# Low parts of the up-projection's weights made by accumulating DMAs instead of GpSimd subtractions

## The chip, the core and the metric

The kernel runs on one core of a Trainium2 chip. Time is the device time of one execution in microseconds (us). The core's engines are TensorE (PE in the profile; its weight loads are PEld), VectorE (DVE), ScalarE (ACT), GpSimd (POOL) and SyncE (SP). They run side by side and wait for each other on semaphores. SBUF is the memory on the core, PSUM holds the results of TensorE.

## What is computed

One layer of a decoder trunk for a prompt of 512 tokens and 8 single tokens, so 520 columns of activations. The part that the change touches is the feed-forward network at its end:

```python
def conv_ffn(h, w_up, conv_w, conv_b, w_down, buf):
    z = h @ w_up                                   # (tokens, 2048) @ (2048, 2 * 5632)
    zp = jnp.concatenate([buf.astype(z.dtype), z], axis=1)
    zc = conv_b + sum(zp[:, j:j + T] * conv_w[j] for j in range(CONV_W))
    g, a = jnp.split(zc, 2, axis=-1)
    y = (jax.nn.silu(g) * a) @ w_down              # (tokens, 5632) @ (5632, 2048)
    return y, zp[:, -(CONV_W - 1):]
```

Ahead of it stand a projection of the normed input, three mixers (a gated MLP, an attention with a window, an mLSTM memory) and an output projection. All arrays are float32.

## The kernel before

**Products in two parts.** TensorE multiplies in the rounded format fp32r. To keep the precision, both sides are split: `whi` is the weight rounded, `wlo` what is left (`raw - whi`), and `h2_hi` and `h2_lo` are the same for the activations. A product is then three: hi x hi, hi x lo of the activations, and lo of the weights x hi (`tile_mm`, line 507; its matmuls have line 514).

**Units and quarters.** An up unit is 128 columns of `w_up`: 2048 x 128 weights, 1 MB. SP loads it into one of the two slots of `raw` (`load_pair`, line 2139 and `load_after`, line 2254). A unit has four quarters of 128 x 512 weights each. `whi` and `wlo` have room for four quarters, a ring: quarter k of each unit stands in place k. Quarter k takes the rows 4c + k of the 16 blocks of 128 rows (`rawq`, a strided view). For each quarter

- ScalarE waits until TensorE has read the place (`w_used`) and writes `whi` (`q_hi`, line 1034, which raises `w_hi`),
- GpSimd waits for `w_hi` and writes `wlo = raw - whi` (`up_split`, line 2107, or `split_pairs`, line 2070; both raise `w_lo`),
- TensorE waits for `w_lo` and runs 24 matmuls of 128 x 260 (`up_mm`): 3 products x 4 blocks x 2 halves of the columns.

A down unit is a block of `w_down` worked in seven pieces of 12 matmuls (`down_unit`, line 913). ScalarE (line 1360) and GpSimd (line 2115) prepare its pieces in the same ring, some of them from `sums` that VectorE makes of the raw blocks (line 1863).

**Order.** The 5632 hidden channels go in 11 groups. Group 0 has eight up units. Groups 1 to 9 are a loop, each with eight up units of its own and the four down units of the group before, in the order `SEQ`. The last group has an order of its own, `SEQ_LAST`, and its down units at the end.

```python
SEQ = ("u0", "u1", "d0", "u2", "d1", "u3", "d2", "u4", "d3", "u5", "u6", "u7")
```

Each unit of this order uses the slot of `raw` given by its place, even or odd. A unit's load is started when the low parts of the unit two places ahead of it are made, because GpSimd is the last reader of `raw`. Seven pieces do not divide by four, so behind a down unit the ring is shifted: place 0, which quarter 0 of the next up unit needs, was last used by the fifth piece, place 1 by the sixth and place 2 by the seventh.

ScalarE and VectorE also do the convolution, the gate and the splitting of the gated activations between the quarters, at places that a table in `ffn_group_act` (`due`) fixes: `start_g` (line 1338), `start_a` (line 1343), `silu`, `gated_hi`, `mixed_hi`.

## Time and profile before

| | before |
|---|---|
| median of 2 runs | 2183.91 us (2182.3 to 2185.52) |
| the profiled execution's span | 2180.7 us |
| TensorE matmuls | 2158.9 us busy, 99% |
| VectorE | 1332.5 us, 61% |
| ScalarE | 820.2 us, 38% |
| GpSimd | 1153.8 us, 53% |
| DMA | 213.66 MB, 34.5% of the 16 engines' span on the main queue |

The busy time of an engine is the time in which it runs instructions. Matmuls are pipelined and their ends are modelled, so two that follow each other overlap in the records; the distance between their starts is the better measure. A line of a group gives its count, its busy time with the mean of one in ns, and the idle time just ahead of its instructions with what ended it. The times in the timeline are from the span's start.

### The profile page before, as it was taken

To read this page: it belongs to the slowest core of one execution; us is meant where nothing else is said; L and a number is where in the kernel's file an instruction comes from. 1 tells how busy PE (TensorE), PEld (TensorE's weight loads), DVE (VectorE), ACT (ScalarE), POOL (GpSimd) and SP (SyncE) were. 2 spreads that over 40 slices of the span, in tenths; PEclk is the share of its full clock that TensorE was granted. 3 is DMA by queue.
4 is the path that set the end of the run, shared out by engine and by line. 5 is a ranking of instruction groups with operands and counts; after the bars stand their busy time and mean duration, and the time that the engine had idled before them with its cause. 6 is when DMAs were issued, how large, how long until landed. Compare 5 with 4: busy or idle time off the path is not lost.

```text
span 2180.7 us, 45547 instructions
## 1 busy us (share of the span) xinstructions
PE 2158.9 (99%) x17888; PEld 2103.8 (96%) x17888; DVE 1332.5 (61%) x1872; ACT 820.2 (38%) x1394; POOL 1153.8 (53%) x868
## 2 busy tenths in 40 slices
PE   7999999999999999999999999999999999999999
PEld 7999988988899999999999999999999999999999
DVE  6122347266643577676785767767677676867765
ACT  5223342255444333333333333333333333333331
POOL 5443333332244457566565765656667575665652
PEclk9999999999999999999999999999999999999999
DMA  7532233752232423323333333233423333333323
GB/s 221 139 91 68 76 75 81 112 158 67 64 88 67 120 78 107 101 84 105 89 96 98 96 98 96 86 96 89 117 77 103 91 96 98 96 96 91 105 81 124
DMA packets 325112, 213.66 MB, mean 98 GB/s; under 512 B 12760, under 2 KB 299473, under 8 KB 324113
## 3 DMA queue, kind: packets, MB, share of 16 engines
q1 hardware_dynamic: 322153, 211.28, 34.5%
q10 hardware_dynamic: 2880, 1.26, 0.3%
q8 instruction: 58, 0.95, 0.2%
q14 instruction: 21, 0.17, 0.0%
HBM read 201.38 MB, written 11.49 MB: 98 GB/s over the span
## 4 chain that ended last, share of the span: by engine, by line
PE 92%; issue 3%; POOL 2%; ACT 1%; DMA 1%; DVE 1%; POOLq 0%; SPq 0%; ACTq 0%; DVEq 0%
PE ps L514 57%; PE ps L913 18%; PE ps L791 8%; PE ps L893 2%; POOL wlo L2070 1%; PE ps L831 1%; PE ps L851 1%; PE ps L841 1%; DMA xtok<-in_x_prompt 0%; PE ps L632 0%; ACT act_hi L1065 0%; DMA raw<-in_w_in 0%; PE ps L478 0%; PE ps L989 0%; PE ps L642 0%
## 5 line engine op out<-in xcount | busy, mean ns | idle before, releaser
L2107 POOL TENSOR_TENSOR wlo<-raw,whi 128x512 fp32r<-128x512 f32 x336 | 467.5, 1399 | 356.9 <-ACT whi L1034 345.2
L1034 ACT ACTIVATE whi<-raw 128x512 fp32r<-128x512 f32 x552 | 340.6, 629 | 727.7 <-PE ps L514 475.5
L2070 POOL TENSOR_TENSOR wlo<-raw,whi 128x512 fp32r<-128x512 f32 x200 | 259.6, 1300 | 443.0 <-ACT whi L1034 443.0
L514 PE MATMUL ps<-h_hi,whi 128*128 128x260 f32 x2816 | 395.7, 283 | 0.0
L514 PE MATMUL ps<-h_lo,whi 128*128 128x260 f32 x2816 | 393.8, 282 | 0.0
L514 PE MATMUL ps<-h_hi,wlo 128*128 128x260 f32 x2816 | 393.2, 282 | 0.0
L514 PEld LDWEIGHTS ps<-h_hi,whi 128*128 128x128 f32 x2816 | 360.9, 188 | 0.4
L514 PEld LDWEIGHTS ps<-h_lo,whi 128*128 128x128 f32 x2816 | 360.8, 188 | 0.0
L514 PEld LDWEIGHTS ps<-h_hi,wlo 128*128 128x128 f32 x2816 | 360.6, 188 | 0.0
L2115 POOL TENSOR_TENSOR wlo<-sums,whi 128x512 fp32r<-128x512 f32 x160 | 215.1, 1344 | 159.6 <-ACT whi L1360 154.8
L1360 ACT ACTIVATE whi<-sums 128x512 fp32r<-128x512 f32 x160 | 101.2, 632 | 269.5 <-PE ps L514 256.7
L913 PE MATMUL ps<-g_hi,whi 128*128 128x260 f32 x1120 | 179.3, 282 | 1.2 <-DVE qacc L1845 1.0
L913 PE MATMUL ps<-g_lo,whi 128*128 128x260 f32 x1120 | 180.4, 283 | 0.0
L2115 POOL TENSOR_TENSOR wlo<-raw,whi 128x512 fp32r<-128x512 f32 x120 | 172.7, 1440 | 13.6 <-ACT whi L1360 8.0
L913 PE MATMUL ps<-g_hi,wlo 128*128 128x260 f32 x1120 | 179.0, 282 | 0.0
L913 PEld LDWEIGHTS ps<-g_hi,whi 128*128 128x128 f32 x1120 | 152.6, 188 | 1.6 <-ACT whi L1034 1.2
L913 PEld LDWEIGHTS ps<-g_lo,whi 128*128 128x128 f32 x1120 | 153.8, 188 | 0.0
L913 PEld LDWEIGHTS ps<-g_hi,wlo 128*128 128x128 f32 x1120 | 153.0, 188 | 0.0
L514 PE MATMUL ps<-act_hi,whi 128*128 128x260 f32 x960 | 141.4, 290 | 0.7 <-POOL wlo L2070 0.7
L1893 DVE TENSOR_TENSOR za<-ps,rs 128x520 f32<-128x520 f32 x44 | 30.8, 700 | 178.8 <-PE ps L514 178.8
L514 PE MATMUL ps<-act_lo,whi 128*128 128x260 f32 x960 | 135.5, 284 | 4.0 <-DVE act_lo L1486 2.4
L514 PEld LDWEIGHTS ps<-act_hi,whi 128*128 128x128 f32 x960 | 124.4, 189 | 10.8 <-issue 9.2
(363 smaller groups left out, 3054.9 us busy)
## 6 DMA issues: line engine op xcount, KB each, us to landing
raw<-in_w_up SPq DMA_DIRECT2D x88, 1024.0 KB, 5.8
raw<-in_w_down SPq DMA_DIRECT2D x44, 1024.0 KB, 5.0
raw<-in_w_in SPq DMA_DIRECT2D x30, 1024.0 KB, 5.6
raw<-in_w_out SPq DMA_DIRECT2D x64, 256.0 KB, 3.8
x_spill<-xT SPq DMA_DIRECT2D x1, 4160.0 KB, 16.1
xtok<-in_x_prompt SPq DMA_DIRECT2D x4, 1024.0 KB, 8.4
out_y_prompt<-ytok SPq DMA_DIRECT2D x3, 1024.0 KB
xT<-x_spill SPq DMA_DIRECT2D x1, 2860.0 KB, 9.4
```

The lines of the kernel that those rows point to most:

```text
L514: mm = nc.tensor.matmul(ps[:, bank + h, 0:NH], w[:, k, c, :], x[:, 4 * c + k, h * NH:(h + 1) * NH], start=(k == 0 and kind == 0 and c == 0 ...
L791: mm = nc.tensor.matmul(ps[:, b + h, 0:NH], w[:, k, c, :], x[:, p, 4 * half + c, h * NH:(h + 1) * NH], start=(half == 0 and kind == 0 and ...
L831: mm = nc.tensor.matmul(ps[:, 4 + r, lo:256], zT[64 * r:64 * r + 64, Z_BQ + u, i * P:(i + 1) * P], keys[:, (i - 1) * P + lo:(i + 1) * P], ...
L841: t = nc.tensor.transpose(ps[:, 6, (2 * r + kb) * P:(2 * r + kb + 1) * P], sx[:, n % 4, r, kb * P:(kb + 1) * P], ident[:])
L893: mm = nc.tensor.matmul(ps[:, b + h, 0:NH], w[:, k, c, :], x[:, h, E_SLOT[c], :], start=(kind == 0 and c == 0), stop=(kind == 2 and c == 3))
L913: mm = nc.tensor.matmul(ps[:, bank + g, 0:NH], w[:, k, 2 * i + g, :], x[:, i, BLOCKS[p], :], start=(kind == 0 and i == 0), stop=(kind == 2 ...
L1034: nc.scalar.activation(whi[:, k, :, :], rawq(k, slot), ACT.Copy)\
L1360: nc.scalar.activation(ring(whi, p % 4), down_weights(p, slot), ACT.Copy).then_inc(w_hi, 1)
L1893: tt(halves(z[:, 2:]), pair(bank), halves(rs2[:]), mult).then_inc(z_free, 1)
L2070: nc.gpsimd.tensor_tensor(wlo[:, k, :, :], rawq(k, u), whi[:, k, :, :].bitcast(F32), ALU.subtract).then_inc(w_lo, 1)
L2107: nc.gpsimd.tensor_tensor(wlo[:, k, :, :], rawq(k, u % 2), whi[:, k, :, :].bitcast(F32), ALU.subtract).then_inc(w_lo, 1)
L2115: nc.gpsimd.tensor_tensor(ring(wlo, k), down_weights(p, slot), ring(whi, k).bitcast(F32), ALU.subtract).then_inc(w_lo, 1)
```

## The change

For the up units u1 to u7 of group 0 and of the nine loop groups, the low part is made in another way. ScalarE writes the rounded quarter into `whi` and the same quarter, rounded and negated, into `wlo` (`signed_hi`). GpSimd then raises `w_lo` by a nop and issues a DMA that adds the raw quarter onto `wlo` in SBUF (`up_add`). Each of the four places has its own semaphore `low_added[k]` for the landing. TensorE waits for it ahead of the quarter, and SP waits for all four before it loads over that slot of `raw`. u0 of each group, the last group and all down units keep the subtraction on GpSimd.

The quarter of these units is now four neighbouring blocks (`raw4`, contiguous in each row of SBUF, 2 KB) instead of every fourth one; `tile_mm` takes the blocks of the activations to match (`four_by_k`). To have semaphores for it, four others are merged with those of the input's loads (`X_LOADED`); this moves no instruction.

```diff
+    low_added = [sem(f"low_added{k}") for k in range(4)]
...
+    def raw4(k, s):
+
+        return raw[:, s, 4 * k * P:4 * k * P + 4 * P].rearrange("p (c n) -> p c n", c=4)
...
-    sems = {}
+    X_LOADED = 16
+    sems = {"kc_in": x_in[0], "vc_in": x_in[1], "b_in": x_in[2], "c_in": x_in[3]}
...
-                                              x[:, 4 * c + k, h * NH:(h + 1) * NH],
+                                              x[:, 4 * k + c if four_by_k else 4 * c + k, h * NH:(h + 1) * NH],
...
-        def up_mm(q0, bank, before=None):
+        def up_mm(q0, bank, before=None, added=None):
             for k in range(4):
                 pe.wait_ge(w_lo, q0 + (k + 1))
                 if before is not None:
                     before(k)
-                tile_mm(k, bank, whi, wlo, h2_hi, h2_lo)
+                if added is not None:
+                    pe.wait_ge(low_added[k], added)
+                tile_mm(k, bank, whi, wlo, h2_hi, h2_lo, four_by_k=added is not None)
...
+        def signed_hi(q, k, slot, landed):
+
+            if k == 0:
+                act.wait_ge(raw_in[slot], landed)
+            act.wait_ge(w_used, q + 1)
+            nc.scalar.activation(whi[:, k, :, :], raw4(k, slot), ACT.Copy)
+            nc.scalar.activation(wlo[:, k, :, :], raw4(k, slot), ACT.Copy, scale=-1.0).then_inc(w_hi, 1)
...
+        def up_add(q, slot):
+
+            for k in range(4):
+                pool.wait_ge(w_hi, q + (k + 1))
+                begun(pool)
+                pool.engine_nop().then_inc(w_lo, 1)
+                nc.gpsimd.dma_start(wlo[:, k, :, :].bitcast(F32), raw4(k, slot), accum_op=ALU.add).then_inc(low_added[k], 16)
...
+        up_split(4 * U_FFN, 0)
+        for u in range(1, U_GRP):
+            up_add(4 * (U_FFN + u), u % 2)
...
-                (down_split if name[0] == "d" else up_split)(q0 + Q_AT[name], at % 2)
+                (down_split if name[0] == "d" else up_add if at else up_split)(q0 + Q_AT[name], at % 2)
...
+                if with_down and older[0] == "u" and older != "u0":
+                    begun(sp)
+                    for k in range(4):
+                        sp.wait_ge(low_added[k], low_count(grp, int(older[1])))
+                        begun(sp)
```

On ScalarE, in the loop behind the down unit d0, before (line 1360 is the last piece of d0, line 1034 the quarters of u2, line 1343 a step of the convolution):

```order
L1360 ACTIVATE whi<-raw 128x512 [waits w_used]
L1033 REGISTER_ALU [waits raw_in1]
L1034 ACTIVATE whi<-raw 128x512 [waits w_used]
L1343 ACTIVATE ca<-za,cpar 128x520 [waits f_za]
L1033 REGISTER_ALU
L1034 ACTIVATE whi<-raw 128x512 [waits w_used]
```

And of the changed kernel at the same place (lines 1395 and 1396 are the two instructions of `signed_hi`):

```order
L1373 ACTIVATE whi<-raw 128x512 [waits w_used]
L1394 REGISTER_ALU [waits raw_in1]
L1395 ACTIVATE whi<-raw 128x512 [waits w_used]
L1396 ACTIVATE wlo<-raw 128x512
L1356 ACTIVATE ca<-za,cpar 128x520 [waits f_za]
L1394 REGISTER_ALU
L1395 ACTIVATE whi<-raw 128x512 [waits w_used]
L1396 ACTIVATE wlo<-raw 128x512
```

The second instruction of each quarter stands directly behind the first and ahead of the step of the convolution.

On GpSimd, at the same place in the loop, before (line 2115 is the last piece of a down unit, line 2107 the quarters of the up unit behind it):

```order
L2114 REGISTER_ALU
L2115 TENSOR_TENSOR wlo<-raw,whi 128x512 [waits w_hi]
L2106 REGISTER_ALU
L2107 TENSOR_TENSOR wlo<-raw,whi 128x512 [waits w_hi]
L2106 REGISTER_ALU
L2107 TENSOR_TENSOR wlo<-raw,whi 128x512 [waits w_hi]
```

And now (line 2134 is the nop that raises `w_lo`, line 2135 the DMA):

```order
L2152 REGISTER_ALU
L2153 TENSOR_TENSOR wlo<-raw,whi 128x512 [waits w_hi]
L2132 REGISTER_ALU
L2134 ISA [waits w_hi]
L2135 DMA wlo<-raw 128x512
L2132 REGISTER_ALU
L2134 ISA [waits w_hi]
L2135 DMA wlo<-raw 128x512
```

A nop and a DMA stand where one subtraction stood.

On TensorE, the start of the up unit behind the down unit, before (line 913 is the last piece of the down unit, line 514 the quarters):

```order
L913 MATMUL ps<-g_hi,wlo 128x260 x3
L967 REGISTER_ALU
L877 REGISTER_ALU [waits z_free,d_ev]
L514 MATMUL ps<-h_hi,whi 128x260 [waits w_lo]
L514 MATMUL ps<-h_hi,whi 128x260 x7
L514 MATMUL ps<-h_lo,whi 128x260 x8
L514 MATMUL ps<-h_hi,wlo 128x260 x8
```

And now:

```order
L925 MATMUL ps<-g_hi,wlo 128x260 x3
L979 REGISTER_ALU
L887 REGISTER_ALU [waits z_free,d_ev]
L891 ISA [waits w_lo]
L524 MATMUL ps<-h_hi,whi 128x260 [waits low_added0]
L524 MATMUL ps<-h_hi,whi 128x260 x7
L524 MATMUL ps<-h_lo,whi 128x260 x8
L524 MATMUL ps<-h_hi,wlo 128x260 x8
```

The wait for the landing stands ahead of the first of the 24 matmuls; the eight that read `wlo` are the last.

## Rows read from the trace of the kernel before

**Rows 1.** The page's part 1: engine, busy us, share of the span, instructions

```profile
PE 2158.9 (99%) x17888; PEld 2103.8 (96%) x17888; DVE 1332.5 (61%) x1872; ACT 820.2 (38%) x1394; POOL 1153.8 (53%) x868
```

**Rows 2.** Windows: stretch, length, busy PE PEld DVE ACT POOL, clock, DMA share, GB/s

```profile
700.00:1900.00 1200.00, 1200.00 (x10047) 1198.18 (x10047) 840.68 (x1015) 445.11 (x711) 736.18 (x532) 1.00 0.33 95
```

**Rows 3.** Groups by line and form, 700 to 1900 us

```profile
L2107 POOL TENSOR_TENSOR wlo<-raw,whi 128x512 fp32r<-128x512 f32 x268 | 374.1, 1404 | 275.9 <-ACT whi L1034 265.8
L514 PE MATMUL ps<-h_hi,whi 128*128 128x260 f32 x2384 | 335.1, 283 | 0.0
...
L1034 ACT ACTIVATE whi<-raw 128x512 fp32r<-128x512 f32 x295 | 180.1, 628 | 326.5 <-PE ps L514 211.2 <-PE ps L913 106.6 <-DMA raw<-in_w_up 6.5
```

**Rows 4.** Timeline of TensorE, end of d0 and start of u2: start, us, instruction

```profile
1084.75 0.64 PE L913 MATMUL ps<-g_hi,whi 128*128 128x260 f32 x4
1085.23 0.64 PE L913 MATMUL ps<-g_lo,whi 128*128 128x260 f32 x4
...
1086.19 0.64 PE L913 MATMUL ps<-g_hi,whi 128*128 128x260 f32 x4
...
1087.61 1.12 PE L514 MATMUL ps<-h_hi,whi 128*128 128x260 f32 x8
1088.57 1.12 PE L514 MATMUL ps<-h_lo,whi 128*128 128x260 f32 x8
```

**Rows 5.** Timeline of ScalarE at the same place

```profile
1084.95 0.63 ACT L1034 ACTIVATE whi<-raw 128x512 fp32r<-128x512 f32 x1 [2.24 <-PE ps L913]
1085.49 0.81 ACT L1343 ACTIVATE ca<-za,cpar 128x520 f32<-128x520 f32 x1
...
1087.81 1.16 ACT L1034 ACTIVATE whi<-raw 128x512 fp32r<-128x512 f32 x2 [0.80 <-PE ps L913]
```

**Rows 6.** Timeline of GpSimd, VectorE and SP's queue at the same place

```profile
1084.24 0.37 SPq L2254 DMA_DIRECT2D raw<-in_w_down  x1
...
1085.66 5.86 POOL L2107 TENSOR_TENSOR wlo<-raw,whi 128x512 fp32r<-128x512 f32 x4 [1.58 <-ACT whi L1034]
...
1089.27 1.10 DVE L1863 TENSOR_TENSOR sums<-raw 128x512 f32<-128x512 f32 x1 [0.66 <-DMA raw<-in_w_down]
...
1091.68 0.37 SPq L2254 DMA_DIRECT2D raw<-in_w_up  x1
```

**Rows 7.** Windows of 1 us there; the last three numbers: clock, DMA share, GB/s

```profile
1085.00:1086.00 1.00, 1.00 (x11) 1.00 (x10) 0.70 (x1) 1.00 (x2) 0.34 (x1) 1.00 0.64 63
...
1087.00:1088.00 1.00, 1.00 (x11) 1.00 (x10) 0.27 (x2) 0.20 (x2) 0.91 (x1) 1.00 1.03 401
```

**Rows 8.** Timeline of TensorE: in u0 of the next group, and at its u1's start

```profile
1059.56 1.12 PE L514 MATMUL ps<-h_hi,whi 128*128 128x260 f32 x8
1060.52 1.11 PE L514 MATMUL ps<-h_lo,whi 128*128 128x260 f32 x8
...
1065.98 1.23 PE L514 MATMUL ps<-h_hi,whi 128*128 128x260 f32 x8
```

**Rows 9.** Timeline of ScalarE and of GpSimd, first quarters of that u1

```profile
1060.80 1.14 ACT L1034 ACTIVATE whi<-raw 128x512 fp32r<-128x512 f32 x2
...
1061.49 2.73 POOL L2107 TENSOR_TENSOR wlo<-raw,whi 128x512 fp32r<-128x512 f32 x2 [5.47 <-ACT whi L1034]
```

**Rows 10.** DMA issues: tensors, queue, count, KB each, median us to landing

```profile
raw<-in_w_up SPq DMA_DIRECT2D x88, 1024.0 KB, 5.8
...
xT<-x_spill SPq DMA_DIRECT2D x1, 2860.0 KB, 9.4
bst<-bias_rows SPq DMA_DIRECT2D x32, 64.0 KB, 2.0
xT<-x_spill SPq DMA_DIRECT2D x1, 1300.0 KB, 6.1
```

**Rows 11.** Windows of 5 us, 20 to 40 us: the first and the sum

```profile
20.00:25.00 5.00, 4.41 (x63) 2.94 (x54) 3.81 (x5) 5.00 (x9) 3.33 (x3) 1.00 1.09 217
...
sum 20.00, PE 16.03 PEld 13.47 DVE 18.78 ACT 19.98 POOL 15.79; mean PE 4.01 PEld 3.37 DVE 4.69 ACT 5.00 POOL 3.95
```

More of the change, by code:

```diff
@@ L505, in unit_mm, with tile_mm @@
                 tile_mm(k, bank, whi, wlo)
-        def tile_mm(k, bank, w_h, w_l, x_h=None, x_l=None, ready=None):
+        def tile_mm(k, bank, w_h, w_l, x_h=None, x_l=None, ready=None, four_by_k=False):
             x_h, x_l = x_h or act_hi, x_l or act_lo
@@ L936, in turn_params, with up_units @@
             t.then_inc(s("par_turn"), 1)
-        def up_units(q0, use0, j, before=None, params=None):
+        def up_units(q0, use0, j, before=None, params=None, i=None):
             for u in range(2):
                 pe.wait_ge(z_free, use0 + (2 * j + u + 1))
-                up_mm(q0 + 4 * u, 2 * u, before if u == 0 else None)
+                up_mm(q0 + 4 * u, 2 * u, before if u == 0 else None, None if i is None or 2 * j + u == 0 else low_count(i, 2 * j + u))
                 if before is not None and u == 0:
@@ L967, in _ @@
                     pe.wait_ge(s("d_ev"), ev + 5)
-                    up_unit(m, l0 + two * L_TWO + L_AT[f"u{m + 2}"], use0 + two * 2 + (m + 3))
+                    up_unit(m, l0 + two * L_TWO + L_AT[f"u{m + 2}"], use0 + two * 2 + (m + 3),
+                            i * (16 * (U_GRP - 1)) + two * 32 + low_count(0, m + 2))
             begun(pe)
             for u in (6, 7):
-                up_unit(u, l0 + L_AT[f"u{u}"], use0 + (u + 1))
+                up_unit(u, l0 + L_AT[f"u{u}"], use0 + (u + 1), low_count(i, u))
         def turn_tail():
@@ L1375, in last_hi, with added @@
             nc.scalar.activation(e_half(g_hi, j), halves(ems[j][:]), ACT.Copy).then_inc(s("g_hi"), 1)
+        def signed_hi(q, k, slot, landed):
[4 more added lines that the diff above has]
+            nc.scalar.activation(wlo[:, k, :, :], raw4(k, slot), ACT.Copy, scale=-1.0).then_inc(w_hi, 1)
         def ffn_group_act(q0, pair0, grp, with_down, ends=False):
+            def added(u):
+                return not ends and u < (len(SEQ) if with_down else U_GRP)
             nonlocal n_group
@@ L1412, in ffn_group_act @@
                     far = back if k < 3 else 0
-                    if m is None:
+                    if m is None and added(u):
+                        signed_hi(q0 + (at_piece + far), k, u % 2, landed)
+                    elif m is None:
                         q_hi(q0 + (at_piece + far), k, u % 2, landed)
@@ L2131, in _, with load_pair @@
         sp.dma_start(wg_raw[:], w_in[:, COL_G:COL_G + 8].rearrange("(c p) n -> p c n", p=P)).then_inc(wg_in, 16)
-        def load_pair(sources, split, down=False):
+        def load_pair(sources, split, down=False, group=None):
             for u in range(2):
@@ L2138, in load_pair @@
                     sp.wait_ge(w_lo, split + 4 * u)
+                if group is not None and group[u][1]:
+                    begun(sp)
+                    for k in range(4):
+                        sp.wait_ge(low_added[k], low_count(*group[u]))
+                        begun(sp)
                 sp.dma_start(unit_dst(u, down), sources[u]).then_inc(raw_in[u], 16)
@@ L2253, in load_after @@
                 sp.wait_ge(w_lo, split + 4 + l_at[older] + (LOWS if older[0] == "d" else 4))
+                if with_down and older[0] == "u" and older != "u0":
+                    begun(sp)
+                    for k in range(4):
+                        sp.wait_ge(low_added[k], low_count(grp, int(older[1])))
+                        begun(sp)
                 sp.dma_start(unit_dst(at % 2, name[0] != "u"), unit).then_inc(raw_in[at % 2], 16)
             if not with_down:
-                load_pair(up(0), split)
+                load_pair(up(0), split, group=[(grp - 1, 6), (grp - 1, 7)] if grp else None)
             if isinstance(grp, int) and grp == 0:
@@ L2265, in load_group @@
             if with_down:
-                load_pair(up(0), split)
+                load_pair(up(0), split, group=[(grp - 1, 6), (grp - 1, 7)])
                 for at in range(2, len(SEQ)):
@@ L2273, in load_group @@
                 for j in range(1, GC):
-                    load_pair(up(j), split + 8 * j)
+                    load_pair(up(j), split + 8 * j, group=[(0, 2 * j - 2), (0, 2 * j - 1)])
         load_group(0, 0, 4 * U_FFN - 4, False)
```

26 lines of the change are left out of this document (14 added, 12 removed).

## The prediction, made before the changed kernel had run

> **What bounds the kernel now.** I read the engine totals first: TensorE is busy 99% of the span, GpSimd 53% [rows 1]. Then the stretch from 700 to 1900 us, nearly all up- and down-projection: TensorE shows 1200.00 busy us of 1200, at the full granted clock of 2.4 GHz [rows 2]. A busy matmul row can hide a wait, so I look at starts in the order of time: blocks of four matmuls start 0.48 us apart in a down unit, blocks of eight 0.96 us apart in an up unit, also across the changes of quarter and of unit [rows 4]. That is 0.1195 us a matmul everywhere. A quarter of an up unit (24 matmuls) takes 2.87 us, a piece of a down unit (12) 1.435 us, and there is no hole. The groups of instructions agree: the matmuls of line 514 have 0.0 us of idle before them, while GpSimd's subtraction at line 2107 waits 275.9 us for ScalarE [rows 3]. So GpSimd's work here is hidden, and taking it away returns nothing. While GpSimd subtracts, from 1085.66 on, the blocks of eight stand 0.96 us apart (1087.61, 1088.57), and so they do at 1059.56 and 1060.52, where GpSimd was idle (its wait of 5.47 us ended at 1061.49) [rows 4, 6, 8, 9]. TensorE isn't slowed by it.
>
> **The change part by part.**
>
> *GpSimd loses 280 subtractions.* u1 to u7 of group 0 and of nine loop groups, 10 x 7 x 4 = 280, at 1404 ns [rows 3]: 393 us of GpSimd time, all under TensorE's matmuls. Worth 0. VectorE may run some operations faster beside an idle GpSimd, but it has 30% of its time left there [rows 2] and TensorE doesn't wait for it. Worth 0.
>
> *ScalarE gains 280 instructions* of 0.63 us [rows 3], 176 us. It is busy 445 of 1200 us [rows 2]; 0 in volume, but the second one stands ahead of the add in each chain. Two such instructions back to back take 1.16 us [rows 5], so that is what the pair costs.
>
> *TensorE's waits.* One more wait a quarter. Down pieces have up to three waits for 12 matmuls and still start at 1.435 us [rows 4]: the extra instruction costs 0. What is waited for is the question, since the new wait stands ahead of the whole quarter, not ahead of its last third, where the low part is read.
>
> *The place that is tight: quarter 0 of an up unit behind a down unit.* Its slot in the ring is free when the fifth of the seven pieces is done, at 1084.75; TensorE wants the quarter at 1087.61, two short pieces later [rows 4]. Slack 2.86 us. Now: ScalarE writes the high part at 1084.95 (0.63 us) [rows 5], GpSimd subtracts from 1085.66 [rows 6] for 1.4 us [rows 3], ready at 1087.06: 0.55 us to spare. After: ScalarE's pair from 1084.95 to 1086.11, GpSimd's issue 0.08 us later (as 1085.58 to 1085.66 now), at 1086.19; then the time X from the issue until the sum has landed and TensorE sees it (0.1 us, estimate, as between other engines' rows). Ready at 1086.29 + X, so the stall is X - 1.32 us. It comes 4 times (u2 to u5) in each of 9 loop groups, 36 times; group 0 has no down units and the last group keeps the subtraction.
>
> *X.* No DMA from GpSimd and no accumulating one is in this trace. From below: 64 KB into the same memory land in 2.0 us; an add moves 256 KB, and its 192 KB more at the slope from that row to the 1 MB load (5.8 us) [rows 10], 3.8/960 us a KB, make 2.8 us. From above: the 1 MB row itself, 5.8 us, more bytes than the add's two reads and one write (768 KB). A line through the two large contiguous reads (1300 KB 6.1, 2860 KB 9.4 [rows 10]) gives 3.9 us for 256 KB and 4.4 us for 512 KB. Against the low end speaks the neighbour: SP starts the 1 MB load for the next down unit at 1084.24, and the 16 DMA engines are busy 0.64 of the time from 1085 and 1.03 from 1087 [rows 6, 7], just when the add would run. I take X = 4.4: stall 3.1 us, 36 x 3.1 = 111 us. The low end gives 36 x 1.5 = 53, the high end 36 x 4.5 = 161.
>
> The Trainium skill, DMA: Bandwidth & Descriptors, section "Anatomy of one DMA - SWDGE (gpsimd) path", fits a GpSimd-issued DMA as 2.0 us plus bytes over 436 GB/s: 2.6 us for 256 KB (estimate from the page), by which the sum would be 36 x 1.3 = 46 us. No run here shows it yet.
>
> *Next quarters of the same unit.* Quarter 1: slot free at 1086.19, ScalarE behind its first pair and line 1343 (0.81 us): pair to about 1088.1, ready at 1088.3 + X; quarter 0 was ready at 1086.3 + X. Two us apart against 2.87 of matmuls: no second stall, unless GpSimd's issue itself holds it over 2.87 us.
>
> *Up units behind up units* (u1, u6, u7, and group 0) have three quarters of slack, 8.6 us, less 1.4 for ScalarE and the handing on: safe up to X = 7. One exception: u1 in the loop, where ScalarE comes late, at 1060.80, because it waited for VectorE's gate. Its pair ends at 1061.94, ready at 1062.1 + X, wanted at 1066.0 [rows 8, 9]: a stall of X - 3.9, with 4.4 0.5 us, nine times: 4 us.
>
> *SP* now also waits for the four sums before it loads into the slot of an up unit. It is moved behind the adds' landing, some 3 to 4 us; the load of a down unit (tight: VectorE waits 0.66 us for it, to 1089.27 [rows 6]) isn't behind that wait, since it replaces a down unit. The next up load starts at 1091.68 now [rows 6], for a unit that TensorE wants after this unit's rest and a whole down unit, at 1087.61 + 11.5 + 10.0 = 1109.1. 0.
>
> *Sum:* 2180.7 (the profiled span) + 111 + 4 = 2295.7. The runs' median lies 3.2 us above the span: **2299 us**, 5.3% slower.
>
> **The rivals.**
>
> *A. Forecast: 36 exposed landings, X from 2.8 to 5.8.* 2237 to 2362 us (the top with u1: 9 x 1.9 = 17). Chance 0.62.
>
> *B. Hidden or nearly so (the other side: not slower).* The place is the same, the point is X: at 1.3 nothing is left, at 2.5 the loss is 36 x 1.2 = 43 us, 2%. For it: 64 KB land in 2.0 us [rows 10] and the add never touches the far memory. Against: the load beside it [rows 6, 7] and three passes over the data. With X = 2.2 it gives 2184 + 32 = 2216. Chance 0.16, of which nothing shorter than before: TensorE has no hole to close [rows 2, 4]. The Trainium skill's fit above lies just over its edge.
>
> *C. The issue is slow: a far larger X.* GpSimd must make the adds' descriptors while VectorE and the loads are busy; with X = 8 the stalls are 36 x 6.7 = 241, u1 9 x 4.1 = 37, the other up-after-up units 2 x 9 + 7 of them about 1 us each, 25: 2487 us. For it: VectorE works 840 of 1200 us [rows 2], and four adds follow each other at 1.2 to 2 us. Against: all those transfers at 5.8 us or less for 1 MB [rows 10]. Chance 0.18. The Trainium skill, SBUF - State Buffer, section "SBUF: two separate sides", says GpSimd cannot write the descriptors while VectorE runs a copy in its two-port mode, so that such a DMA seems blocked; here that would be the small copies of 10 columns only, and no row shows what mode they run in.
>
> *D. The clock falls.* With 36 stalls TensorE could be granted 1.2 GHz for some of the time. Against: from 20 to 40 us it is busy 16 of 20 us with holes, at clock 1.00 [rows 11]. Chance 0.02, slower than C.
>
> *E. Faster by over 2%.* It would need 44 us out of matmuls that already follow each other at 0.1195 us. Chance 0.02.
>
> **How the numbers follow.** Within 2% (about what a measurement of this kernel can tell from no change) is B: 0.16. Slower is A, C and D: 0.82. Faster 0.02. The range leaves out the lower half of B (below X = 2.2: 2215) and the upper half of C. At its top X = 6.4: 36 x 5.1 + 9 x 2.5 = 206, so 2390. 2215 to 2390.
>
> **What would show it.** TensorE idle in the changed profile some 36 times between 800 and 2010 us, at the first matmul of u2 to u5, released by a DMA on wlo, about 3 us each; none at u6 and u7; little at u1. GpSimd's subtractions fall by 393 us and ScalarE's time rises by 176, each pair of its instructions 1.16 us. The loads of up units start 3 to 4 us later. The blocks of eight stay at 0.96 us. Wrong would be: no waits (B), waits also at quarters 1 to 3 or at u6 and u7 (C), another clock (D), or blocks of another length (the layout of the quarter then matters, which I cost at nothing).

## The result, and the profile after the change

The changed kernel takes 2362.44 us (median of 2 runs, 2362.06 to 2362.82) against 2183.91 us. The ratio is 1.0817, 95% interval 1.0786 to 1.0849: 178.5 us, 8.2% slower. The forecast was 2299 us within 2215 to 2390. The direction and the range held. The loss was 178.5 us where I had worked out 115.

The page's parts 1 and 3 (engine, busy us, share of the span; DMA queue, packets, MB, share) of the changed kernel:

```profile
PE 2219.6 (94%) x17888; PEld 2154.7 (91%) x17888; DVE 1121.8 (48%) x1872; ACT 964.3 (41%) x1674; POOL 980.5 (42%) x868
...
q0 software_dynamic: 40320, 73.42, 18.1%
q8 instruction: 94, 1.54, 0.3%
```

Two things stand here. TensorE's matmuls are the same 17888 as in [rows 1], yet its busy time grew from 2158.9 to 2219.6 us: some matmuls became slower. And the queue that brings TensorE its instructions moved 94 packets. In the kernel before it moved 58 (the same line of its page says 58, 0.95 MB).

The same stretch as [rows 2] and the groups that answer to [rows 3]:

```profile
700.00:1900.00 1200.00, 1103.83 (x8805) 1093.78 (x8803) 561.43 (x886) 507.94 (x852) 500.61 (x464) 0.96 0.58 134
```

```profile
L524 PE MATMUL ps<-h_hi,whi 128*128 128x260 f32 x2816 | 414.0, 291 | 118.8 <-DMA wlo<-raw 106.4
...
L2135 POOL DMA_DIRECT2D wlo<-raw x280 | 241.8, 867 | 482.8 <-ACT wlo L1396 456.3
...
L1396 ACT ACTIVATE wlo<-raw 128x512 fp32r<-128x512 f32 x280 | 172.1, 614 | 0.0
```

The first matmuls of the quarters (line 524, which was 514) had no idle time before them; now it is 118.8 us. The mean granted clock of the stretch fell from 1.00 to 0.96. What TensorE waited for (columns: us in all, times, longest), and the time from GpSimd's issue of an add until it had landed:

```profile
PE ps L524 <- DMA wlo<-raw: 106.4, 40, 3.6
PE ps L524 <- issue: 9.3, 3, 3.2
...
PE ps L524 <- POOL wlo L2141: 2.9, 1, 2.9
```

```profile
DMA to landing us min/median/max: 3.2/3.8/7.2
```

**One hole in full.** The place answers to that of [rows 4 to 7], two units later in the pass: the end of d2 and the start of u4. Timeline of all engines in the changed kernel (start, us, engine, instruction):

```profile
1176.74 0.63 ACT L1395 ACTIVATE whi<-raw 128x512 fp32r<-128x512 f32 x1 [2.24 <-PE ps L925]
...
1177.28 0.62 ACT L1396 ACTIVATE wlo<-raw 128x512 fp32r<-128x512 f32 x1
...
1178.49 0.87 POOL L2135 DMA_DIRECT2D wlo<-raw  x1 [2.63 <-ACT wlo L1396]
...
1178.93 0.64 PE L925 MATMUL ps<-g_hi,wlo 128*128 128x260 f32 x4
...
1181.12 0.69 DVE L1889 TENSOR_TENSOR sums<-raw 128x512 f32<-128x512 f32 x1 [0.73 <-DMA raw<-in_w_down]
...
1182.32 2.10 PE L524 MATMUL ps<-h_hi,whi 128*128 128x260 f32 x8 [2.75 <-DMA wlo<-raw]
...
1184.22 1.94 PE L524 MATMUL ps<-h_lo,whi 128*128 128x260 f32 x8
...
1185.95 1.94 PE L524 MATMUL ps<-h_hi,wlo 128*128 128x260 f32 x8
...
1187.69 1.46 PE L524 MATMUL ps<-h_hi,whi 128*128 128x260 f32 x8
...
1188.99 1.11 PE L524 MATMUL ps<-h_lo,whi 128*128 128x260 f32 x8
```

The last four matmuls of the down unit start at 1178.93, so TensorE wants the quarter at 1179.41. It starts at 1182.32: a hole of 2.91 us, of which the record shows 2.75, since the ends of matmuls are modelled 0.16 us long. The first block behind a hole also takes some 0.1 us more to its successor (1131.65 to 1132.72 below, against 0.96), so I count 0.27 us beside each recorded wait.

What I had not foreseen begins behind the hole. The next blocks of eight stand 1.90, 1.73, 1.74 and 1.30 us apart instead of 0.96. The granted clock in windows of 1 us (the number ahead of the last two):

```profile
1181.00:1182.00 1.00, 0.00 (x0) 0.00 (x0) 0.84 (x2) 0.79 (x2) 0.75 (x2) 0.82 0.99 176
1182.00:1183.00 1.00, 0.68 (x3) 0.68 (x4) 1.00 (x2) 0.00 (x0) 0.82 (x2) 0.50 1.13 195
...
1189.00:1190.00 1.00, 1.00 (x11) 1.00 (x10) 0.00 (x0) 0.00 (x0) 0.93 (x1) 1.00 1.09 307
```

The clock went from 2.4 to 1.2 GHz inside this hole, some 0.7 us before its end, and the blocks behind ran at half speed until it came back. Most falls come a little later: of the 26 in this run, 7 begin inside a hole and the others up to 1.5 us after TensorE has started again. The clock doesn't fall at every hole:

```profile
1131.65 1.23 PE L524 MATMUL ps<-h_hi,whi 128*128 128x260 f32 x8 [2.63 <-DMA wlo<-raw]
1132.72 1.12 PE L524 MATMUL ps<-h_lo,whi 128*128 128x260 f32 x8
```

**Holes that wait for nothing.** At four of the eight edges between passes of the loop over groups TensorE stands idle though its data are ready. One edge, and the DMA queues in the window from 1245 to 1252 us:

```profile
1246.31 1.12 PE L524 MATMUL ps<-h_hi,wlo 128*128 128x260 f32 x8
1250.60 2.10 PE L524 MATMUL ps<-h_hi,whi 128*128 128x260 f32 x8 [3.17 <-issue]
```

```profile
q8 instruction: 2, 0.03, 3.3%
```

In this window the queue of instruction loads moves packets, in the middle of a loop whose body TensorE had run before. The kernel before has none between 907 and 1983 us.

**The sum of the loss,** 2360.0 - 2180.7 = 179.3 us of span. The first quarters of u2 to u5: 36 holes, 102.5 us recorded and 36 x 0.27 beside them, 112.2. Three small ones at u1, 0.15 to 0.39 us: 1.7. One in group 0: 3.3. Four loop edges: 12.2 recorded and 1.1 beside them, 13.3. Blocks at half clock, over their length at full clock: 47.0. Together 177.5, and 1.8 us is left unexplained. So two terms are missing in my sum: the clock, and the loop edges.

### The profile page after: what moved, and what is told of

Read it like the earlier page. It is cut to its first block, busy times and chain, and to the rows that moved or that the text cites. A ratio compares the mean times of both kernels' runs of the same rounds, so it can differ in the third digit from the quotient of the medians.

```text
span 2360.0 us, 47033 instructions
## 1 busy us (share of the span) xinstructions
PE 2219.6 (94%) x17888; PEld 2154.7 (91%) x17888; DVE 1121.8 (48%) x1872; ACT 964.3 (41%) x1674; POOL 980.5 (42%) x868
## 3 DMA queue, kind: packets, MB, share of 16 engines
q8 instruction: 94, 1.54, 0.3%
## 4 chain that ended last, share of the span: by engine, by line
PE 79%; DMA 8%; issue 6%; POOL 3%; ACT 2%; DVE 1%; POOLq 0%; SPq 0%; ACTq 0%; DVEq 0%
PE ps L524 52%; PE ps L925 12%; PE ps L801 8%; DMA wlo<-raw 7%; PE ps L905 2%; POOL wlo L2096 1%; ACT wlo L1396 1%; POOL wlo L2141 1%; PE ps L841 1%; PE ps L861 1%; PE ps L851 1%; DMA xtok<-in_x_prompt 0%; PE ps L642 0%; ACT act_hi L1078 0%; DMA raw<-in_w_in 0%
## 5 line engine op out<-in xcount | busy, mean ns | idle before, releaser
L524 PE MATMUL ps<-h_hi,whi 128*128 128x260 f32 x2816 | 414.0, 291 | 118.8 <-DMA wlo<-raw 106.4
L524 PEld LDWEIGHTS ps<-h_hi,whi 128*128 128x128 f32 x2816 | 374.1, 195 | 129.1 <-DMA wlo<-raw 111.7
L2135 POOL DMA_DIRECT2D wlo<-raw x280 | 241.8, 867 | 482.8 <-ACT wlo L1396 456.3
L524 PE MATMUL ps<-h_lo,whi 128*128 128x260 f32 x2816 | 413.3, 291 | 0.0
L524 PE MATMUL ps<-h_hi,wlo 128*128 128x260 f32 x2816 | 410.1, 290 | 0.0
L2096 POOL TENSOR_TENSOR wlo<-raw,whi 128x512 fp32r<-128x512 f32 x168 | 217.6, 1297 | 391.5 <-ACT whi L1047 391.5
L524 PEld LDWEIGHTS ps<-h_lo,whi 128*128 128x128 f32 x2816 | 379.2, 197 | 0.0
L524 PEld LDWEIGHTS ps<-h_hi,wlo 128*128 128x128 f32 x2816 | 378.1, 196 | 0.0
L1047 ACT ACTIVATE whi<-raw 128x512 fp32r<-128x512 f32 x272 | 170.3, 630 | 438.8 <-PE ps L524 311.6
L1395 ACT ACTIVATE whi<-raw 128x512 fp32r<-128x512 f32 x280 | 175.3, 626 | 283.2 <-PE ps L524 189.7
L2153 POOL TENSOR_TENSOR wlo<-raw,whi 128x512 fp32r<-128x512 f32 x120 | 156.5, 1304 | 133.3 <-ACT whi L1373 130.2
L1396 ACT ACTIVATE wlo<-raw 128x512 fp32r<-128x512 f32 x280 | 172.1, 614 | 0.0
L2141 POOL TENSOR_TENSOR wlo<-raw,whi 128x512 fp32r<-128x512 f32 x88 | 117.4, 1337 | 122.9 <-ACT whi L1047 122.2
L1373 ACT ACTIVATE whi<-raw 128x512 fp32r<-128x512 f32 x120 | 75.9, 632 | 219.1 <-PE ps L524 156.6
```

The source lines that it names most:

```text
L524: mm = nc.tensor.matmul(ps[:, bank + h, 0:NH], w[:, k, c, :], x[:, 4 * k + c if four_by_k else 4 * c + k, h * NH:(h + 1) * NH], start=(k = ...
L1047: nc.scalar.activation(whi[:, k, :, :], rawq(k, slot), ACT.Copy)\
L1373: nc.scalar.activation(ring(whi, p % 4), down_weights(p, slot), ACT.Copy).then_inc(w_hi, 1)
L1395: nc.scalar.activation(whi[:, k, :, :], raw4(k, slot), ACT.Copy)
L1396: nc.scalar.activation(wlo[:, k, :, :], raw4(k, slot), ACT.Copy, scale=-1.0).then_inc(w_hi, 1)
L2096: nc.gpsimd.tensor_tensor(wlo[:, k, :, :], rawq(k, u), whi[:, k, :, :].bitcast(F32), ALU.subtract).then_inc(w_lo, 1)
```

## Experiments

Three questions: is the loss all in the 36 first quarters and not in the adds as such; what brings the clock down; what are the holes at the loop edges. The kernel before was run beside each set: 2182.29, 2182.51 and 2182.55 us.

### Where an add costs, and where not

**The same sums, made by GpSimd itself.**

```diff
-                nc.gpsimd.dma_start(wlo[:, k, :, :].bitcast(F32), raw4(k, slot), accum_op=ALU.add).then_inc(low_added[k], 16)
+                nc.gpsimd.tensor_tensor(wlo[:, k, :, :], raw4(k, slot), wlo[:, k, :, :].bitcast(F32), ALU.add).then_inc(low_added[k], 16)
```

> The changed kernel, but the raw quarter is added onto the negated one by a GpSimd instruction (128x512, 1.3 us) instead of a DMA; the order of all waits, ScalarE's pair and TensorE's program stay. Theory 1 (the loss is the landing of the add behind down units, and what the holes bring with them): the add is ready at 1086.19 + 1.3 + 0.1 = 1087.6, just when TensorE wants it, so hardly a hole, clock 1.00, and a span of 2181 to 2195 us; the 94 instruction packets of the DMA queue q8 fall back to 58. Theory 2 (the clock and the instruction loading come from the changed TensorE program or ScalarE's second write): clock 0.976 and 94 packets stay, span 2230 us or more. Theory 3 (the contiguous quarter makes matmuls slower): blocks of eight over 0.96 us.

Measured: 2206.23 us (4 runs, 2195.81 to 2215.63), ratio 1.0122 [1.0096, 1.0148]. Instruction loads, in the profile of the fastest of them:

```profile
q8 instruction: 67, 1.10, 0.2%
```

ScalarE's second instruction, the other layout of the quarters, the new waits of TensorE and SP are all still there, and of 178 us some 24 are left. In the profiled run there is one hole over 1 us between 800 and 2010, at a loop edge, and no fall of the clock. So the rest of the loss comes with the transfer as the thing waited for. But the median lies above what theory 1 said, and the packets did not fall to 58. The profiled run is 13.1 us over the span of before. By the starts of its matmuls the edge is 2.2 of them; at the 36 first quarters behind down units TensorE starts late by 2.4 us in all and then has 0.1 us more between the first matmul and the second, 3.9 us in all; the rest is not taken apart. The spread of 20 us between executions is unlike the kernel before; a varying number of loop edges, described below, could make such a spread, but only one execution has a profile.

**The wait moved to where the low part is read,** ahead of the third block of eight instead of the first.

```diff
-                    pe.wait_ge(low_added[k], added)
+                    def late(k, kind):
+                        if kind == 2:
+                            pe.wait_ge(low_added[k], added)
```

> The changed kernel with TensorE's wait for the landing ahead of the eight matmuls that read the low part instead of ahead of all 24. They come 16 x 0.1195 = 1.9 us later, so theory 1 (the hole is the landing alone) makes the 36 holes 2.9 - 1.9 = 1.0 us and takes away those at the other units: 36 us of holes. If the clock falls because of long holes, it stays at 1.00: span about 2220 us. If it falls because the adds are there, whatever the holes (rival), another 45 us: about 2265 us with a mean clock of 0.976.

Measured: 2229.79 us (2229.47 to 2230.11), ratio 1.0216 [1.0195, 1.0236].

```profile
PE ps L524 <- DMA wlo<-raw: 34.2, 37, 1.5
```

```profile
1148.03 1.23 PE L524 MATMUL ps<-h_hi,wlo 128*128 128x260 f32 x8 [1.04 <-DMA wlo<-raw]
```

The same transfers, waited for 1.92 us later in the work: 36 holes of 0.6 to 1.5 us, none followed by a fall of the clock, and 58 packets of instructions. 34.2 and 37 x 0.27 are 44.2 us, the span grew by 47.4. The holes are then nearly the whole loss.

**Only the first quarter behind a down unit goes back to the subtraction;** 244 of the 280 adds stay.

```diff
+                if plain and k == 0:
+                    nc.gpsimd.tensor_tensor(wlo[:, k, :, :], raw4(k, slot), whi[:, k, :, :].bitcast(F32),
+                                            ALU.subtract).then_inc(w_lo, 1)
+                    continue
```

> The changed kernel, but the first quarter of u2 to u5 in the loop groups gets its low part by GpSimd's subtraction as before; the other three quarters of these units, and all quarters of u1, u6, u7 and of group 0, keep the accumulating DMA (244 of 280 remain). Theory 1, all the loss sits in 36 waits of the first quarter behind a down unit and in what follows from them: no hole and no slow clock, 2184 to 2196 us. Rival, the adding DMAs cost something themselves (GpSimd's issue of 0.87 us, their traffic of 16 queues, the layout of the quarters): a good part of the 178 us stays, in proportion 244 of 280, so 2300 us or more. Between them, 2200 to 2220, would say that quarter 1 becomes late now, since it is next in the chain.

Measured: 2248.25 us (4 runs, 2239.5 to 2250.03), ratio 1.029 [1.0266, 1.0315]. That is 52 us over what theory 1 said.

```profile
PE ps L526 <- DMA wlo<-raw: 38.0, 40, 2.8
```

```profile
1126.03 1.12 PE L526 MATMUL ps<-h_hi,wlo 128*128 128x260 f32 x8
...
1128.01 1.22 PE L526 MATMUL ps<-h_hi,whi 128*128 128x260 f32 x8 [0.86 <-DMA wlo<-raw]
```

The hole moved one quarter on. 1126.03 is the last block of quarter 0, and quarter 1 is late by 0.86 us, most times by just that. In the changed kernel the hole at quarter 0 had covered it. The terms: 38.0 + 40 x 0.27 = 48.8, two loop edges of 3.2 and what stands beside them (76 packets) 6.9, slow blocks 6.1; 61.8 of 64.7 us. So the loss was not only in the first quarters: they were the longest of a row of late ones, and the one that sets the time.

**All four quarters behind a down unit go back;** the adds stay behind up units, 136 of 280. In each place where the program chooses:

```diff
+    ADD_LOOP, ADD_0 = [1, 6, 7], [1, 2, 3, 4, 5, 6, 7]
...
-                (down_split if name[0] == "d" else up_add if at else up_split)(q0 + Q_AT[name], at % 2)
+                (down_split if name[0] == "d" else up_add if int(name[1]) in ADD_LOOP else up_split)(q0 + Q_AT[name], at % 2)
```

> The changed kernel, but u2 to u5 of the loop groups get all their low parts by GpSimd's subtraction as before, with the layout of before; the adding DMA stays for u1, u6 and u7 of the loop groups and for u1 to u7 of group 0: 136 of 280 adds, all behind an up unit. Theory 1, an add costs time only where less than some 4.3 us lies between the ring slot coming free and the first matmul: here there are 8.6 us, so no waits but a few tenths at u1, clock 1.00, and 2184 to 2190 us plus 3.4 us for each loop edge at which TensorE loads its instructions again (0 to 4 of them): 2184 to 2204 us. Rival, every add costs something on the path: 136 of 280 of 178 us, 87 us, so about 2270 us.

Measured: 2190.97 us (6 runs, 2189.7 to 2194.91), ratio 1.0035 [1.0022, 1.0048].

```profile
723.84 2.07 PE L528 MATMUL ps<-h_hi,whi 128*128 128x260 f32 x8 [2.80 <-DMA wlo<-raw]
```

Half of all adds cost 8.4 us, by the profile four holes of 6.1 us together and one fall of the clock. The first hole, at 723.84, is in group 0, where the changed kernel has one too, at 722.19 (3.00 us). There the chain is another one. ScalarE in the changed kernel, and SP's queue in the window from 709 to 711 us:

```profile
716.02 0.63 ACT L1395 ACTIVATE whi<-raw 128x512 fp32r<-128x512 f32 x1 [6.67 <-DMA raw<-in_w_up]
...
709.43 0.73 SPq L2182 DMA_DIRECT2D raw<-in_w_up  x1
```

And in the kernel before, in windows from 714 and from 709 us:

```profile
715.44 1.15 ACT L1034 ACTIVATE whi<-raw 128x512 fp32r<-128x512 f32 x2 [6.51 <-DMA raw<-in_w_up]
...
709.55 2.31 SPq L2139 DMA_DIRECT2D raw<-in_w_up  x2
```

ScalarE waits for the load of the raw weights, and it did so before: SP started that load at 709.55 us there and at 709.43 in the changed kernel, so SP's new wait does not delay it. TensorE wants the quarter at about 719.2 in both. The 3.7 us from 715.44 were enough for a subtraction and are too few for ScalarE's pair and a landing.

**The neighbour's load held back** until the first add has landed.

```diff
+                if with_down and older[0] == "d":
+                    begun(sp)
+                    sp.wait_ge(low_added[0], low_count(grp, int(seq[at - 1][1])))
+                    begun(sp)
```

> The changed kernel, but SP holds back the 1 MB load that it starts beside the first add of u2 to u5 (that of the next down unit, and that behind the last) until that first add has landed. Theory 1, the add's landing of 3.8 us is lengthened by the load beside it: landing near the shortest one seen, 3.2 us, so each of 36 holes is 0.5 us shorter, with fewer clock falls: 2310 to 2345 us, unless the later load makes a down unit late. Rival, the landing is made of fixed steps and not of contention: landings stay at 3.8 us, the waits at 106 us, and the time at 2355 us or more, since the load comes 4 us later where VectorE waited 0.66 us for it.

Measured: 2450.6 us (2435.15 and 2466.05), ratio 1.1226 [1.1144, 1.1308].

```profile
PE ps L524 <- DMA wlo<-raw: 124.1, 51, 4.6
PE ps L925 <- DVE zg L1919: 19.6, 7, 4.6
```

The holes did what theory 1 said: at the 36 first quarters they are 83.3 us in all, 2.31 us on average, against 102.5 and 2.85 in the changed kernel. At u5, where they were 3.2 to 3.6 us, they are 2.2 to 2.4; at u2 to u4 they are mostly 0.3 to 0.45 us shorter. So the 1 MB load beside it costs the add about 0.5 us of its landing. The time failed both expectations: the later load makes other places late. Down pieces wait for VectorE, which waits for the load (232.9 us at its sums of the down weights), and sums near the end of a pass come up to 4.6 us late.

### What brings the clock down

**No DMA, a hole from GpSimd's own work.** In the kernel before, the subtraction for the first quarter behind a down unit is done three times instead of once, then four times in the next.

```diff
+                if k == 0 and first is not None:
+                    for n in range(2):
+                        nc.gpsimd.tensor_tensor(wlo[:, k, :, :], rawq(k, u % 2), whi[:, k, :, :].bitcast(F32),
+                                                ALU.subtract).then_inc(chain_p, 1)
+                        pool.wait_ge(chain_p, first + n)
```

> The kernel before, no DMA add: GpSimd makes the first quarter of each up unit behind a down unit three times (two more subtractions of 1.3 to 1.4 us, each with a wait on itself), 36 times. Spare time there is 0.55 us, so a hole of 2.1 to 2.4 us: 76 to 86 us. Clock by holes: some falls, fewer than in the changed kernel, span 2260 to 2290 us. Clock by DMA adds: clock 1.00, span 2257 to 2267 us.

Measured: 2278.65 us, ratio 1.044 [1.0419, 1.0461].

```profile
PE ps L514 <- POOL wlo L2112: 69.6, 36, 1.9
```

```profile
1111.69 1.87 PE L514 MATMUL ps<-h_hi,whi 128*128 128x260 f32 x8 [1.93 <-POOL wlo L2112]
1113.36 1.94 PE L514 MATMUL ps<-h_lo,whi 128*128 128x260 f32 x8
```

```profile
1136.97 1.22 PE L514 MATMUL ps<-h_hi,whi 128*128 128x260 f32 x8 [1.93 <-POOL wlo L2112]
1138.03 1.12 PE L514 MATMUL ps<-h_lo,whi 128*128 128x260 f32 x8
```

The clock around the first of these two:

```profile
1111.00:1112.00 1.00, 0.31 (x2) 0.31 (x3) 0.67 (x1) 0.00 (x0) 1.00 (x2) 1.00 0.00 0
1112.00:1113.00 1.00, 1.00 (x7) 1.00 (x6) 0.96 (x2) 0.00 (x0) 1.00 (x1) 0.50 0.00 0
```

36 equal holes of 1.93 us; ten are followed by slow blocks (15.1 us in all), the others not. TensorE starts again at 1111.69 at the full clock, and the clock falls at 1112.00; in nine of the ten it falls only when TensorE already works again. No DMA engine is busy in these two microseconds. 69.6 + 36 x 0.27 + 15.1 = 94.4 of 95.8 us of span.

With `range(3)`, three more subtractions:

> As the kernel with two more subtractions, with three: holes of 3.5 to 3.9 us, 36 x = 126 to 140 us. Clock by holes: falls as in the changed kernel or more, 45 us or more on top, span 2350 to 2390 us and clock 0.97. Clock by DMA adds: clock 1.00 and 2307 to 2321 us. TensorE's instruction loading (packets of q8): stays at 58 if it comes from the changed program, goes up if it comes from holes.

Measured: 2379.69 us (2367.2 to 2392.17), ratio 1.0903 [1.0835, 1.0971].

```profile
PE ps L514 <- POOL wlo L2112: 126.9, 36, 3.6
```

```profile
1131.73 2.10 PE L514 MATMUL ps<-h_hi,whi 128*128 128x260 f32 x8 [3.60 <-POOL wlo L2112]
```

35 falls, and 66 us in slow blocks between 800 and 2010, 76 over the whole span. The instruction loads stay at the 58 packets of before, and there is no add anywhere. This kernel, with a wait and no transfer, loses in the same two parts as the changed one: 126.9 + 36 x 0.27 = 137 us of holes and 76 of slow blocks. That is 213 for a loss of 209.7; the 0.27 beside a hole and the slow block behind it are in part the same time.

**The hole filled.** In the changed kernel, TensorE computes the quarter's first eight matmuls three times for nothing ahead of the wait.

```diff
+                if fill and k == 0:
+                    for n in range(3):
+                        for c in range(4):
+                            for h in range(2):
+                                nc.tensor.matmul(ps[:, bank + h, 0:NH], whi[:, k, c, :],
+                                                 h2_hi[:, 4 * k + c, h * NH:(h + 1) * NH], start=(c == 0), stop=(c == 3))
                 if added is not None:
                     pe.wait_ge(low_added[k], added)
```

> The changed kernel, but ahead of the wait for the first quarter's sum in u2 to u5 of the loop groups TensorE computes that quarter's first eight matmuls three times for nothing (24 matmuls, 2.87 us at full clock; the accumulation starts anew behind them, so the output stays the same). The wait of about 2.9 us is then filled with work. Theory 1, the clock falls because TensorE stands idle: the holes shrink to under 0.5 us, the clock stays at 1.00, and only the length of the holes remains on the path: 2362 less the 45 us of slow blocks, 2310 to 2322 us. Theory 2, the clock falls because of the transfers or of power drawn elsewhere at that moment: the slow blocks come back, 2355 us or more. If filling moved nothing else, the waits for the sums fall from 106 us to under 20.

Measured: 2337.03 us (4 runs, 2335.3 to 2341.11), ratio 1.0709 [1.0691, 1.0727]; the changed kernel, run beside it, 2370.47.

```profile
1153.35 3.04 PE L894 MATMUL ps<-h_hi,whi 128*128 128x260 f32 x24
1157.30 1.23 PE L524 MATMUL ps<-h_hi,whi 128*128 128x260 f32 x8 [0.91 <-DMA wlo<-raw]
```

```profile
800.00:1900.00 1100.00, 1074.73 (x8895) 1067.54 (x8894) 538.77 (x845) 470.04 (x789) 483.32 (x442) 1.00 0.58 134
```

Line 894 is the filling. The same adds run at the same time, the quarter starts as late as before or later, and the clock stays up: two falls in place of 25, 1.7 us in slow blocks in place of 38.1 (800 to 2010). Doing nothing useful for 36 x 2.87 = 103 us gave back 33 us. So the falls come with TensorE's idle time, not with the traffic and not with what it waits for. The time is 15 us over the expected 2310 to 2322: 14.1 us of waits for the sums were left, and the longer program loads its instructions at all eight edges (130 packets), which is next.

How often the clock fell behind holes of one length, as the runs show it:

| kernel | holes | recorded length, us | followed by a fall |
|---|---|---|---|
| wait before the last third | 36 | 0.6 to 1.5 | 0 |
| two more subtractions | 36 | 1.93 | 10 |
| load held back, first quarters | 36 | 2.2 to 3.1 | 22 |
| changed kernel, first quarters | 36 | 2.6 to 3.6 | 21 |
| changed kernel once more (below) | 36 | 2.5 to 3.7 | 20 |
| three more subtractions | 36 | 3.3 to 3.6 | 35 |

The length is not all of it. In the first execution of the changed kernel the longest holes, the nine of u5 with 3.2 to 3.6 us, were followed by a fall 3 times, the other 27 18 times; and at the loop edges below, eight holes of 1.8 to 2.4 us had a fall behind each. What decides the single hole is not shown.

The Trainium skill, "TensorE: Matmul & The Clock Gate", section "HAM oscillation - how this bites in real kernels", describes this shape: a wait for a DMA between bursts of matmuls drops the clock, and each burst then starts cold. The runs here agree with it, and show that it needs no DMA and doesn't happen at each hole.

### The holes at the loop edges

**The changed kernel once more.**

> The changed kernel, unaltered, once more. What is open: at four edges of the loop over groups TensorE stood idle some 3 us with all its data ready, and its queue of instruction loads moved 94 packets against 58 in the kernel before. If that belongs to the program it comes again: 94 packets, four such holes, 2358 to 2366 us. If it is chance that a profile catches, the count differs (58 to 94), the holes come at other edges or not at all, and the time moves by about 3.4 us for each. The 36 waits for the sums and the clock falls behind them must return in either case: 100 to 112 us of waits, 95 to 115 us at half clock.

Measured: 2370.47 us (4 runs, 2369.63 to 2376.55), ratio 1.0866 [1.0848, 1.0884].

```profile
PE ps L524 <- DMA wlo<-raw: 108.6, 43, 3.7
```

```profile
q8 instruction: 112, 1.84, 0.4%
```

Six edges this time, not four, and 18 packets more: nine a pass. The hole in group 0 had no fall behind it this time, and there are 25 falls in all. The waits for the sums are as before. Two more edges at about 3.4 us are 6.8 of the 9.2 us between the two spans. What is loaded again is then partly a matter of the single execution.

**The kernel before with a longer program.** 48 empty instructions of TensorE's sequencer in the loop's body, six ahead of each quarter of u6 and u7:

```diff
             for k in range(4):
+                for _ in range(more[k]):
+                    pe.sem_inc(const_made)
                 pe.wait_ge(w_lo, q0 + (k + 1))
```

> The kernel before, with 48 instructions of TensorE's sequencer more in the body of the loop over groups: six empty semaphore increments (on one that nobody waits for any more) ahead of each quarter of u6 and u7. No adds, no holes from them. What is open is why TensorE loads its instructions again at loop edges: 4 and 6 of 8 edges in two executions of the changed kernel, 8 of 8 where its body was 48 instructions longer, none in the kernel before. Theory 1, the size of the loop body decides: 130 packets on the queue of instruction loads instead of 58, eight holes of about 3.2 us at the edges, and 2182 plus 27, about 2205 to 2212 us. Theory 2, the stalls and waits of the adds bring it about: 58 packets, no such hole, and within 2 us of the kernel before.

Measured: 2211.89 us (4 runs, 2207.34 to 2213.44), ratio 1.0126 [1.0108, 1.0143].

```profile
q8 instruction: 130, 2.13, 0.4%
```

```profile
1195.05 1.33 PE L514 MATMUL ps<-h_hi,whi 128*128 128x260 f32 x8 [2.12 <-POOL wlo L2109]
1196.18 1.94 PE L514 MATMUL ps<-h_lo,whi 128*128 128x260 f32 x8
```

58 + 8 x 9 = 130: all eight edges load the body again, with a hole of 1.8 to 2.4 us and a fall of the clock behind each one. Eight edges cost 29 us, 3.6 each. No add is in this program. So the length of the loop's body alone can bring these holes about, and the releaser that the view names (GpSimd's wlo) need not be their cause.

**With 5 more** (two ahead of the first quarter of u6, one ahead of each other):

> The kernel before, with 5 empty sequencer instructions more in TensorE's loop body (two ahead of the first quarter of u6, one ahead of each other): as many as the new waits add to the changed kernel's loop. If the size of the body decides and the kernel before lies just under the edge, some of the 8 loop edges now show instruction loads: 67 to 112 packets, up to 6 holes of 3.2 us, 2185 to 2203 us. If 5 more do not reach it, or the stalls bring it about, 58 packets and 2182 us.

Measured: 2183.12 us (10 runs, 2180.77 to 2184.15), ratio 1.000 [0.999, 1.001].

```profile
q8 instruction: 58, 0.95, 0.2%
```

No load, no hole. But the change adds more than the 5 instructions that the expectation takes for it. It adds 20: counted in the traces from one branch of the loop over groups to the next, with the inner loop's body (two down units and two up units, run twice a pass) once, TensorE's instructions are 1580 in the kernel before and 1600 in the changed one, namely 15 more waits and 5 more register instructions. With the wait moved to the last third the 15 waits need no instruction of their own, and the filling adds 96 to the changed kernel's (48 matmuls and as many weight loads), not 48 as the expectation above has it. All kernels in the order of this count (one or two records can be missing in a count), with the passes loaded again in the profiled execution:

| kernel | TensorE's instructions in the body | passes loaded again, of 8 |
|---|---|---|
| before, two and three more subtractions | 1580 | 0 |
| 5 more | 1585 | 0 |
| wait before the last third | 1585 | 0 |
| adds behind up units only | 1592 | 0 |
| first quarter subtracted | 1598 | 2 |
| changed kernel, twice | 1600 | 4 and 6 |
| GpSimd's sums; load held back | 1600 | 1; 4 |
| 48 more | 1628 | 8 |
| hole filled | 1696 | 8 |

The two columns rise together, whether or not there are adds and stalls: no load up to 1592, some at 1598 and 1600, all eight from 1628 on. What decides the single pass at 1600, and whether the place of the loop in the program matters too, stays open.

The Trainium skill, "Advanced Engine Details and Errata", section "ISA Cache", gives TensorE 128 KB and lines of 16 KB, 256 instructions each; that would be 8 lines, 2048 instructions (an estimate from the page). By it a body of 1600 takes 6.25 lines and lies on seven or eight, so a few dozen instructions more or a shifted start could push it over. The packets of 16 KB each (1.54 MB in 94) agree with the line; no run here shows the size of the whole. The same section says "Only 2 cache lines!", 512 instructions; that doesn't hold here, since the kernel before keeps a body of 1580 from pass to pass without a load.

## Why the prediction was right, and where it failed

**The tight place: right.** Quarter 0 of u2 to u5 in nine loop groups, 36 holes, each released by a DMA on wlo. I had 3.1 us each, 111 us in all; measured are 102.5 + 9.7 = 112.2 us.

**X: right in sum, by luck: two errors cancel.** I took 4.4 us from an issue 0.08 us behind ScalarE's pair. In the hole above ScalarE ends at 1177.90 and TensorE starts at 1182.32; less 0.08 and 0.1 that makes X = 4.2, and the mean hole of 3.12 us makes it 4.4. But GpSimd's record starts 0.59 us behind ScalarE, not 0.08, and the landing takes 3.8 us from there, near the 3.9 that the line through the large reads gave for 256 KB. The fit of the Trainium skill ("DMA: Bandwidth & Descriptors", section "Anatomy of one DMA - SWDGE (gpsimd) path"), 2.6 us for 256 KB, was under the shortest landing seen, 3.2 us; the trace doesn't agree with it, and the 46 us that followed from it were far off.

**Work removed and added, worth 0: right.** GpSimd's busy time fell by 173 us (393 of subtractions less 242 of issues, the other subtractions a little faster), ScalarE's rose by 144, 0.51 us a pair. Neither is in the sum of the loss. VectorE's busy time fell by 211 us, and it too bought nothing. Only "the extra instruction costs 0" was not quite so (the 0.1 us behind a first quarter's first matmul in the kernel with GpSimd's sums), and in its effect on the length of the body it was wrong, see below.

**Next quarters: right in effect, not in reason.** There was no second stall in the changed kernel. But when the first hole was taken away, quarter 1 was late by 0.86 us. By my own numbers it was ready at 1088.3 + 4.4 = 1092.7 and wanted, without a hole, at 1090.5; I compared it with quarter 0 as it would be delayed only.

**Up units behind up units, SP: nearly right.** u1 cost 1.7 us in place of 4, u6 and u7 nothing, and SP's wait nothing: in the hole above the next up load starts 10.8 us behind the down load (1186.81 and 1176.03), where it was 7.4 [rows 6], 3.3 us later, as forecast, and nobody waited for it. Group 0 had one hole, 3.3 us and a slow stretch of 2.6 behind it, where I had put 0. The sum took three quarters of slack for every up unit behind an up unit; here the load of the raw weights left 3.7 us, as it had in the kernel before (715.44 to 719.2). I had looked at the loop only.

**The clock: the step that failed.** "With 36 stalls TensorE could be granted 1.2 GHz for some of the time" was rival D, with a chance of 0.02, set against the forecast as if only one of them could be. In fact it is a consequence of the forecast, and 47.0 us of the loss are it: 21 of the 36 holes, four edges and the one in group 0 are followed by a fall, 26 falls with 105.8 us at half clock. My reason against it was [rows 11], where TensorE is idle for 4 of 20 us at full clock. Such a window gives the sum of the idle time, not the length of one piece, and holes of 0.6 to 1.5 us did leave the clock alone in a run here. The long holes of this forecast were 3.1 us, and for those I had no row.

**The loop edges: not in the sum at all.** 13.3 us. I counted "the extra instruction costs 0" in time and did not ask what the program's length does. The trace of before had the sign of it: the queue of instruction loads, quiet from 907 to 1983 us, in a loop with 1580 of TensorE's instructions in its body. The change made them 1600.

With both terms the sum is 115 + 47 + 13, and 3 for group 0: 178 of the 179.3 us of span.

## What to carry to other kernels

An accumulating DMA in place of an engine's add trades 1.4 us of that engine for about 4.4 us of waiting (0.6 to the issue's record, 3.8 to the landing); it is nearly free where more than that lies between buffer and use (136 adds behind up units cost 8.4 us together), and a hole where less does. That time has to be counted from when the raw data are there, not only from when the place is free. Where a hole of 2 to 4 us in TensorE is forecast, add the half clock behind it (36.5 us behind the 36 here, 1.0 a hole), and put a wait ahead of the part that reads the data, which alone gave back 133 of 178 us (and, by the shorter body, the loop edges with it). And look at TensorE's queue of instruction loads and count the instructions of a long loop's body: here 12 more cost nothing in loads, 20 more brought loads in one to six of eight passes and 48 more in all, at 3.6 us a pass with the clock.

## What the runs showed of the hardware that I had not expected

- The granted clock falls in or just behind a hole of TensorE, mostly when TensorE is already at work again; equal holes of 1.93 us had it 10 times in 36, and longer holes were not always followed by it. Filling the changed kernel's holes with useless matmuls made it 33 us faster.
- The length of TensorE's loop body has a cost that no wait names: 48 empty instructions cost 29 us in a kernel whose engines do the same work.
- VectorE's additions of the down weights (line 1863 before, 1889 after) take 0.69 us where they took 1.10 [rows 6] beside GpSimd's subtractions; over all of them the mean is 0.75 against 1.33. With GpSimd's own sums in place of the DMAs it is 1.48, so it is GpSimd's work that slows them.
